# Feed-forward blocks that begin token-stationary, and a norm tile turned inside the output projection

## The reference

```
def rms_norm(x, g):
    y = x * rsqrt(mean(x * x, axis=-1, keepdims=True) + 1e-6)
    return y * g

def swiglu(h, w_in, w_out):                 # w_in: 1024 x 5632, w_out: 2816 x 1024
    a, b = split(h @ w_in, 2, axis=-1)
    return (silu(a) * b) @ w_out

for l in range(2):
    x = x + 0.5 * rms_norm(swiglu(rms_norm(x, ffn1_norm_pre[l]), ...), ffn1_norm_post[l])
    y = token_mixer(rms_norm(x, mix_norm_pre[l]), ...)       # ends in merged @ w_out
    x = x + rms_norm(y, mix_norm_post[l])
    x = x + 0.5 * rms_norm(swiglu(rms_norm(x, ffn2_norm_pre[l]), ...), ffn2_norm_post[l])
```

## Time and profile before

| | |
|---|---|
| median of 3 runs | 2048.53 us (2047.55 to 2050.34) |
| profiled execution | 2049.0 us |
| its span | 2047.3 us |
| TensorE busy | 1926.9 us, 94% |
| DVE, ScalarE, POOL busy | 1068.4, 899.9, 456.1 us |
| mean granted TensorE clock | 0.944 |

### The profile page before, as it was taken

The page is one execution under the profiler, slowest core; times in us unless marked ns, Lnnn a source line. Parts: engine busy times, 40 slices in busy tenths (PEclk is TensorE's granted clock), DMA queues, the critical chain, the costliest instruction groups (busy, mean ns, idle before and its releaser), DMA issues. The chain is left out here.

```text
span 2047.3 us, 31499 instructions
## 1 busy us (share of the span) xinstructions
PE 1926.9 (94%) x12048; PEld 1678.0 (82%) x12048; DVE 1068.4 (52%) x1887; ACT 899.9 (44%) x1386; POOL 456.1 (22%) x203
## 2 busy tenths in 40 slices
PE   6999999999899979999999999899888988999889
PEld 6999799988599969998999886899877867755665
DVE  7555561336355555554642344655484496651762
ACT  5443442784344444444335862444444433233363
POOL 1000001445100010000004443000066972004730
PEclk9999997999899979999997999899989998599999
DMA  6554446233354434544554324455434542004421
GB/s 275 185 184 184 174 177 241 99 124 124 134 185 184 184 135 179 185 185 170 186 214 156 118 97 150 168 184 186 157 124 149 190 154 93 1 1 151 157 93 52
DMA packets 29913, 311.69 MB, mean 152 GB/s; under 512 B 3312, under 2 KB 3696, under 8 KB 4848
## 3 DMA queue, kind: packets, MB, share of 16 engines
q1 hardware_dynamic: 28944, 307.13, 40.5%
q0 software_dynamic: 864, 3.15, 0.5%
HBM read 309.21 MB, written 1.05 MB: 152 GB/s over the span
## 5 line engine op out<-in xcount | busy, mean ns | idle before, releaser
L732 PE MATMUL psum<-hH,ring_r 128*128 128x256 f32 x2432 | 699.9, 288 | 0.0
L732 PE MATMUL psum<-hH,region_r 128*128 128x256 f32 x2336 | 668.4, 286 | 27.9 <-DVE xs_r L406 12.7
L732 PE MATMUL psum<-xs_r,region_r 128*128 128x256 f32 x2336 | 669.2, 286 | 0.0
L394 ACT ACTIVATE region_r<-ring 128x1024 fp32r<-128x1024 f32 x455 | 475.0, 1057 | 395.9 <-PE psum L732 341.9
L400 POOL TENSOR_TENSOR ring_r<-ring,region_r 128x1024 fp32r<-128x1024 f32 x141 | 344.5, 2466 | 1023.7 <-ACT region_r L394 1023.7
L400 DVE TENSOR_TENSOR ring_r<-ring,region_r 128x1024 fp32r<-128x1024 f32 x314 | 382.1, 1224 | 268.1 <-ACT region_r L394 252.1
L732 PEld LDWEIGHTS psum<-hH,region_r 128*128 128x128 f32 x2336 | 458.0, 196 | 42.6 <-issue 25.5
L732 PEld LDWEIGHTS psum<-hH,ring_r 128*128 128x128 f32 x2432 | 463.5, 191 | 0.0
L732 PEld LDWEIGHTS psum<-xs_r,region_r 128*128 128x128 f32 x2336 | 447.2, 191 | 4.4 <-issue 0.5
L732 PE MATMUL psum<-region_r 128*128 128x512 f32 x704 | 232.1, 392 | 0.0
L732 PE MATMUL psum<-region_r,hH 128*128 128x512 f32 (+3 forms) x512 | 160.4, 351 | 9.4 <-POOL ring_r L400 6.6
(11 more groups left out here) (200 smaller groups left out, 2138.9 us busy)
## 6 DMA issues: line engine op xcount, KB each, us to landing
ring<-in_weights SPq DMA_DIRECT2D x192, 1536.0 KB, 6.4
gpost<-in_posts POOLq DMA_DIRECT2D x6, 512.0 KB, 4.6
cst<-in_const SPq DMA_DIRECT2D x1, 1198.0 KB, 23.1
xs<-in_mem SPq DMA_DIRECT2D x1, 1024.0 KB, 5.6
x<-in_x SPq DMA_DIRECT2D x1, 1024.0 KB, 7.6
out<-x SPq DMA_DIRECT2D x2, 512.0 KB, 2.6
pars<-in_par SPq DMA_DIRECT2D x1, 336.0 KB, 8.0
p<-in_par SPq DMA_DIRECT2D x1, 204.0 KB, 24.8
```

The lines of the kernel that those rows point to most:

```text
L394: eng.activation(unit.high, unit.raw, ACT.Copy).then_inc(h_ready, 1)
L732: ins = pe.matmul(bank, lhsT, rhs, start=start, stop=stop)
```

## The change

The first two gate and up tiles of each block are computed by token tile: the normed tokens are the stationary operand and 512 columns (two gate tiles, two up tiles) move. `rows(i, some)` does this for token tile i. The host packs the first four units of a block accordingly. Gate and up then have tokens in partitions, so the product of Silu and up is turned by two transposes per token tile (`turned`), and DVE splits what comes out (`first_parts`). `first_down(i)` is the down product of hidden tile 0 for token tile i. The semaphore for hL is one per token tile, so that rows(0) does not wait for token tile 1. In first blocks, tile 1 is turned after half of rows(0); in second blocks, tile 0 is turned inside the output projection between kk = 4 and kk = 5 of token tile 1, and tile 1 after rows(0). AHEAD is 4.

(Cut to its core; headings of the hunks are put in words.)

```diff
@@ constants
-AHEAD = 2
+AHEAD = 4
...
@@ Jobs.ffn
+        for i in range(NT):
+            self.add("T", "gT", f, i)
...
@@ input_low (one semaphore per token tile)
-                .then_inc(nL_ready, 1)
+                .then_inc(nL_ready[i], 1)
...
@@ TensorE, ffn
-                norm(("ffn", f), k)
-                parted(k - 1)
+                if f == 0:
+                    norm(("ffn", f), k, [0])
...
-                up(0)
-                up(1)
-                down(0, first=True)
+                both = [Job("ff", f, i) for i in range(NT)]
+
+                def rows(i, some):
+
+                    for kk in some:
+                        unit = Split(at + kk // 2)
+                        if i == 0:
+                            pe.wait_ge(l_ready, unit.count)
+                        if kk % 4 == 0:
+                            pe.wait_ge(nL_ready[i], 2 * (k - 1) + kk // 4 + 1)
+                        if kk == 0:
+                            both[i].wait_empty(pe)
+                        products(both[i].bank, [h[:, i, kk, :] for h in (hH, hL)],
+                                 [w[:, kk % 2 * 512:(kk % 2 + 1) * 512] for w in (unit.high, unit.low)],
+                                 kk == 0, kk == KD - 1, both[i].full if kk == KD - 1 else None)
+                        if i and kk % 2:
+                            used.append(h_room)
+                        if i and kk == 5:
+                            used.append(w_used[at // 3 % SLOTS])
+
+                def turned(i):
+
+                    both[i].wait_emptied(pe)
+                    job = Job("gT", f, i)
+                    job.wait_empty(pe)
+                    for t in range(2):
+                        turn(job.bank[:, t * P:(t + 1) * P], gT[:, i, t * P:(t + 1) * P], job.full if t else None)
+
+                def first_down(i):
+                    Job("gT", f, i).wait_emptied(pe)
+                    unit = Split(at + 4)
+                    pe.wait_ge(l_ready, unit.count)
+                    for half in range(2):
+                        outs[2 * i + half].wait_empty(pe)
+                        products(outs[2 * i + half].bank, [g[:, 0, i * P:(i + 1) * P] for g in (gH, gL)],
+                                 [w[:, half * 512:(half + 1) * 512] for w in (unit.high, unit.low)],
+                                 True, False, h_room if i and half else None)
+
+                rows(0, range(0, 4))
+                if f == 0:
+                    norm(("ffn", f), k, [1])
+                rows(0, range(4, 8))
+                if f == 1:
+                    norm(("ffn", f), k, [1])
+                rows(1, range(0, 4))
+                turned(0)
+                rows(1, range(4, 8))
+                first_down(0)
+                turned(1)
+                first_down(1)

...
@@ TensorE, end of mixer, and project
-                project("mixed", AT_OUT, KD, mergedT, lambda kk: pe.wait_ge(merged, KD * lay[0] + kk + 1))
+                project("mixed", AT_OUT, KD, mergedT, lambda kk: pe.wait_ge(merged, KD * lay[0] + kk + 1),
+                        lambda: norm(("ffn", 1), k + 1, [0]))
...
+            def project(name, at, k, lhs, before, between=None):
+
+                project_rows(name, at, k, lhs, before, 0, range(k))
+                if between is None:
+                    project_rows(name, at, k, lhs, before, 1, range(k))
+                else:
+                    project_rows(name, at, k, lhs, before, 1, range(0, 5))
+                    between()
+                    project_rows(name, at, k, lhs, before, 1, range(5, k))
...
@@ ScalarE, ffn and end of mixer
-                norm_parts(("ffn", f))
+                if f == 0:
+                    norm_parts(("ffn", f))
                 first = U_FFN2 if f else U_FFN1
                 split(first, AHEAD, HIGHS)
                 table(ACT.Silu)
...
                 for i in range(NT):
                     post("mixed", 1.0, [i])
                     norm(k + 1, tiles=[i])
+                    norm_parts(("ffn", 1), [i])
...
@@ DVE, ffn (norm takes tiles now)
-                norm(("ffn", f), k, gain, scale="late" if f else "early")
+                if f == 0:
+                    norm(("ffn", f), k, gain, scale="early")
...
-                if f == 0:
-                    dve.tensor_tensor(hmT, memT, bc(A("gmem"), 2, SEQ), ALU.mult).then_inc(hm_ready, 1)
+                def first_gated(i):
+
+                    job = Job("ff", f, i)
+                    before = lay[0] * (2 * FT) + (f * FT + i)
+                    dve.wait_ge(sil_ready, before + 1)
+                    dve.tensor_tensor(gT[:, i, :], sil[:, i, :], job.bank[:, SEQ:2 * SEQ], ALU.mult).then_inc(job.free, 1)
+
+                def first_parts(i):
+
+                    job = Job("gT", f, i)
+                    before = lay[0] * (2 * FT) + (f * FT + i)
+                    cols = slice(i * P, (i + 1) * P)
+                    job.wait_full(dve)
+                    for t in range(2):
+                        dve.tensor_copy(gH[:, t, cols], job.bank[:, t * P:(t + 1) * P]).then_inc(g_steps, 1)
+                    dve.wait_ge(g_steps, 2 * before + 2)
+                    dve.tensor_tensor(gL[:, :, cols], job.bank[:, 0:SEQ].rearrange("p (t n) -> p t n", t=2),
+                                      gH[:, :, cols].bitcast(F32), ALU.subtract).then_inc(job.free, 1)

...
                 def body(it):
                     for c in range(SLOTS):
-                        gated(c, it)
                         for n in range(3):
                             low_part(dve, first + HIGHS + 3 * c + n, it)
-
+                        gated(2 + c, it)
+
+                first_gated(0)
+                first_parts(0)
+                first_gated(1)
+                first_parts(1)
+                if f == 0:
+                    dve.tensor_tensor(hmT, memT, bc(A("gmem"), 2, SEQ), ALU.mult).then_inc(hm_ready, 1)
                 repeat(dve, (FT - 2) // SLOTS, body)
-                gated(FT - 2)
-                gated(FT - 1)
+
...
@@ DVE, end of mixer
                 for i in range(NT):
                     post("mixed", p, 1, lay[0] + 1, [i])
-                    if i == 0:
-                        scaled(0, k + 1)
+                    scaled(i, k + 1)
+                    norm(("ffn", 1), k + 1, A("g2"), tiles=[i])
...
@@ host packing of the feed-forward weights
-        tiles = [a[0], b[0], a[1], b[1], o[0]]
+        both = [np.concatenate([t[:, k * P:(k + 1) * P] for t in (a[0], a[1], b[0], b[1])], 1) for k in range(KD)]
+        tiles = [np.concatenate(both[k:k + 2], 1) for k in range(0, KD, 2)] + [o[0]]
```

More of the change, by code:

```diff
@@ L549, in build @@
         h_room = sem("h_room")
-        nH_ready, nL_ready = sem("nH_ready"), sem("nL_ready")
+        nH_ready, nL_ready = sem("nH_ready"), [sem(f"nL_ready{i}") for i in range(NT)]
         yH_ready, yL_ready = sem("yH_ready"), sem("yL_ready")
@@ L753, in chunk_round, with norm @@
                 return n // SLOTS
-            def norm(name, k):
-                for i in range(NT):
+            def norm(name, k, tiles=range(NT)):
+                for i in tiles:
                     pe.wait_ge(xs_ready, NT * k + i + 1)
@@ L776, in parted @@
             def parted(k):
-                pe.wait_ge(nL_ready, 4 * (k + 1))
+                for i in range(NT):
+                    pe.wait_ge(nL_ready[i], 2 * (k + 1))
             def products(out, lhs, rhs, start, stop, signal=None):
@@ L820, in up, with down @@
                     used.append(h_room)
-                def down(t, it=0, first=False, last=False):
+                def down(t, it=0, last=False):
                     Job("ff", f, t, plus=2 * it).wait_emptied(pe)
@@ L828, in down @@
                         i, half = j // 2, j % 2
-                        if first:
-                            out_job.wait_empty(pe)
                         products(out_job.bank, [g[:, t % 2, i * P:(i + 1) * P] for g in (gH, gL)],
                                  [w[:, half * 512:(half + 1) * 512] for w in (unit.high, unit.low)],
-                                 first, last, out_job.full if last else h_room if j == 3 else None)
+                                 False, last, out_job.full if last else h_room if j == 3 else None)
@@ L1111, in project_rows @@
                         used.append(w_used[(at + kk // 3) % SLOTS])
-            def project(name, at, k, lhs, before):
-                for i in range(NT):
-                    project_rows(name, at, k, lhs, before, i, range(k))
+            def project(name, at, k, lhs, before, between=None):
[6 more added lines that the diff above has]
+                    project_rows(name, at, k, lhs, before, 1, range(5, k))
             def token_blocks(name, blocks, at):
@@ L1339, in split, with norm_parts @@
                     high_part(act_, u)
-            def norm_parts(name):
-                for i in range(NT):
+            def norm_parts(name, tiles=range(NT)):
+                for i in tiles:
```

(13 more changed lines are left out.)

## The result

Median of four runs 2073.5 us (2072.4 to 2073.8) against 2048.5 us: 1.012 times the time of before, 95% interval 1.0102 to 1.0137. The change costs 25.0 us; 27.7 were forecast. The profiled execution took 2073.3 us, its span is 2071.4, 24.1 longer than before's.

What follows compares the result with a forecast made beforehand. TensorE, busy 94% of the span, was taken as the bound, so its work and gaps counted. 4.0 + 10.0 + 2.2 + 10.0 + 1.5 = +27.7 us on 2048.5 gave 2076 us, range 2066 to 2088.

Steps and rivals of the forecast that it cites:

- Second blocks: Feed-forward blocks f = 1: ScalarE awaits the fourth unit's chunk before tile 0's post norm, TensorE stands 12 us; +10.0 us per layer.
- p: Time the low clock takes from a block's first products: 1.4 to 2.3 us, taken as equal before and after.
- silu(0)'s multiply: Multiply after tile 0's Silu, which turned(0) waits for: done at T + 5.9; in second blocks put at 571.9.
- T: The end of tile 1's transposes, from which silu(0)'s multiply is counted; 565.6 in the second block.
- Rival A: Second blocks: chunk lands before post("mixed") is due, so ScalarE is not held; -4.7 us per block, 2047 us in all; 8%.
- Rival B: Second blocks: TensorE at half clock over all six projection matmuls (+4) and again for rows(1) (+1 net); 2086 us; 10%.
- the wait for silu(0): TensorE's idle time before turned(0) in second blocks: 1.6 us, absorbing most of the loss from rows(1)'s half-clock start.
- First block of layer 0: Start 1.1 us late from two more POOL lows, plus 2.9 us for the block itself; together +4.0 us.
- The wait of first_down(1): TensorE idle behind turned(1) while DVE makes two copies and a subtraction: 1.15 us.
- Passage into layer 1: Four ScalarE highs delay the chain 1.5 us, yet the block starts 0.7 us early; with its +2.9, +2.2 us.
- Rival C: Steady loop: DVE's new order makes each up wait 0.2 to 0.5 us in 80 tiles; 2092 to 2116 us; 3%.
- the tail: Ahead of the even layer: the same four ScalarE highs as at layer 1's passage, with TensorE idle; +1.5 us.

Runs made afterwards that it cites:

- e1: Changed kernel, but in second blocks ScalarE makes three weight highs before tile 0's post norm and the fourth after it, POOL's lows likewise: 2044.2 us, 0.9982 of before.
- e2: Kernel before the change with one edit, AHEAD = 4 instead of 2, none of the new order: 2064.0 us, 1.0082 of before.
- e3: Changed kernel, but in first blocks and the even layer POOL makes two weight lows before norm_low and the other two behind: 2068.7 us, 1.0105 of before.
- e5: Changed kernel with the three reorderings of e1, e3 and e6 together: 2037.0 us, 0.9954 of before.
- e7: As e5, but DVE copies the turned tile out of PSUM in one 256-column copy instead of two of 128: 2038.6 us, 0.9960 of before.
- e4: Changed kernel, but second blocks turn tile 0 behind the whole output projection, the late weight high kept: 2062.3 us, 1.0068 of before.
- e6: Changed kernel, but at each layer's end ScalarE makes two weight highs before the post norm and the other two behind it: 2067.7 us, 1.0102 of before.

## Why the prediction was right

**Second blocks, the deciding step.** Forecast +10.0 each. Measured in layer 0: 13.21 us late at the third tile less 3.56 at the projection, +9.7. The steps, with after's times less 3.56 and the forecast behind them: transposes in the projection 548.7 (548.9); rows(0) 557.0 (557.1); tile 1's transposes 564.8 (564.5); its rows 567.6 (567.5). ScalarE began the high 6.29 us after the load's issue (the forecast had 6.0 to 6.6). The cause was named from one row, SP's issue at 534.49, together with the order of ScalarE's instructions, and e1 and e2 show it. In layer 1 the block cost 8.8 us: 15.8 late before the projection, 24.65 at the last Silu. The 1.2 us less than forecast are mostly on the side of before. From first product to Silu its block there took 8.59 us against 7.76 in layer 0, while after's two took 13.74 and 13.73; p, the low clock's share, was 2.6 us in that block of before and 1.8 in layer 0's.

The forecast's working has a slip here. It has silu(0)'s multiply done at 571.9, where its own T + 5.9 gives 571.5; measured was T + 5.7 (569.41 to 575.10). Without it the block would have come to +9.6.

**Rival A** was priced at 4.7 us gained per second block if the load were not in the way. e1 takes it out of the way and gains 5.2 in layer 0 and 4.7 in layer 1. Its mechanism and price were right, its condition (the slot free 6 us earlier) does not hold in this kernel.

**Rival B** held in part: the rest of the projection took 7.11 us at 554.00 against 5.32 in e1, so the low clock took 1.8 us, against 4 by the rival and about 1 in the forecast, and rows(1) started low once more. The window over rows(1):

```profile
571.00:575.00 4.00, 3.86 (x10) 3.04 (x11) 3.37 (x5) 3.97 (x6) 0.00 (x0) 0.57 0.01 2
```

That loss lies ahead of the wait for silu(0) and is hidden by it for the most part, as forecast: the block's cost came out 0.3 below.

**First block of layer 0: forecast +4.0, measured +5.2.** The start was 1.36 us late (forecast 1.1). The block took 3.8 us more, not 2.9 (the terms as listed add up to 2.8). The step that failed is "p stands on both sides and cancels". From 26.73 to 31.99 twelve matmuls of 512 columns take 5.26 us where 2.77 were due: p is 2.5 us and was 1.4. In layer 1 p is 2.5 against 2.25, and there the block took 2.89 more, as forecast. Layer 1's second block, above, is the same step with the other sign. The wait of first_down(1), put at 1.15 us, is 1.04.

**Passage into layer 1: forecast +2.2 less the block's 2.9, that is a start 0.7 us early; measured: 0.3 us later** (13.5 after 13.2). ScalarE's post norm comes 5.6 us behind the last Silu instead of 4.2: 1.4, forecast 1.5. The missing 1.0 is DVE's residual adds, 2.20 and 1.67 us where before had 1.26 and 1.22, beside POOL's four lows. The prediction charged POOL's lows for their own time and not for what they do to DVE. e3 shows both adds at 1.23 with the other two lows moved away. The Trainium skill (GPSIMD Engine Reference, "Specifications") lists POOL's SBUF interfaces as shared with VectorE, with contention where an instruction of DVE has two SBUF inputs. The rows agree: the residual add reads x and xs, both in SBUF. That entry gives no size, and here it was 0.45 to 0.94 us on 1.26.

**Rival C** is out: between the third tile and the last Silu no block gains or loses more than 0.02 us.

**The sum.** Forecast 4.0 + 10.0 + 2.2 + 10.0 + 1.5 = 27.7. Measured by the same stretches: 5.2, then -1.6 in layer 0's mixer, +9.7, +3.2, -0.6 in layer 1's mixer, +8.8, and -0.5 behind: 24.2, and the spans differ by 24.1. So layer 0's first block and the stretch from its second block to layer 1's third tile were 2.2 us too small in the forecast. Against that stand three things that it had too large or not at all: the two mixers gave back 2.2 us, layer 1's second block was 1.2 us cheaper, and the tail came out 2.0 below its +1.5. That the total is only 2.7 off is in part luck; the 20 us for the second blocks, 18.5 measured, are not.

The mixers. In layer 0 the lateness falls from 5.2 to 3.5 us between 332 and 337 us of before. There TensorE's granted clock is 0.50 in before from 332.1 on, and in after from 339.2 on; the low stretch lasts 30.7 us in before and 27.3 in after. The same window of both kernels, before first:

```profile
332.00:367.00 35.00, 34.09 (x173) 33.12 (x173) 4.84 (x17) 8.41 (x19) 6.25 (x3) 0.56 0.56 218
```
```profile
332.00:367.00 35.00, 34.09 (x191) 33.32 (x190) 3.02 (x13) 9.38 (x19) 6.26 (x3) 0.61 0.64 244
```

TensorE is equally busy in both, with 18 matmuls more in after at a mean clock of 0.61 against 0.56. Whether the change did this is not shown, and e5 and e7 speak against it: their mixers are the same program, and the low stretch in layer 0 lasts 27.3 us in one and 30.7 in the other. Layer 1's mixer gave back 0.6 us (16.4 late, then 15.8).

The tail. The +1.5 us forecast ahead of the even layer is not found at the end. Its products start 2.6 us later than before relative to the last Silu, yet this is gone later in the tail, and at the end 0.5 us less than at that Silu is left. The stretch from the last Silu to the end varies from 570.0 to 576.2 us over the seven experiments, and by 1.9 between e5 and e7, so this last term stays open.

## What to carry to other kernels

Here each engine takes its instructions in program order, so a deeper look-ahead can hold up what is queued behind it, as ScalarE's wait of 14.96 us held up the post norm. Before raising such a count, find the buffer slot that the extra item lands in, the instruction that frees it, and what stands behind the wait for it. If that is a chain that another engine needs, put the extra item behind the chain and keep the depth. Splitting the look-ahead of the second blocks (three, then one) turned a change that cost 25 us into one that gains 4; the two further reorderings bring the gain to 11. Moved work is not free either: the lows that e3 took out of one DVE instruction's way stood in another's at the next place. Where a transpose is put inside a stream of matmuls, the rest of the stream waits with it when its input is late (4.4 us in e4's comparison).

## What the runs showed of the hardware

- An add of DVE with both operands in SBUF, 128x1024, takes 1.23 us, and 1.67 to 2.20 us when it starts while a POOL subtraction of that size runs. It ends 1.08 to 1.09 us after that subtraction (after: POOL's ends at 760.50 and 763.80, the adds' at 761.58 and 764.88; e6: 762.26 and 763.35), nearly as if it began only then. DVE's input lows of 128x512, 0.7 us each alone, ended 0.54 to 0.55 us after POOL's subtraction (e3: 1512.85 and 1513.40, 1515.60 and 1516.14) and took 2.8 us each.
- After a wait of 8.9 us TensorE's 512-column matmuls started 0.43 us apart for 5.26 us, twice their 0.231. The window of after reads 1.00 there, because its clock has no record before 32.0 us. In e1 the same twelve matmuls run at the same pace, and there the clock is recorded as 0.50 from 18.0 to 31.7 us. In after's layer 1 the same pace goes with 0.50. The windows, after, e1 and after again:

```profile
26.70:32.00 5.30, 5.27 (x13) 4.04 (x14) 0.00 (x0) 0.00 (x0) 1.77 (x2) 1.00 0.52 193
...
26.70:32.00 5.30, 5.16 (x13) 4.04 (x14) 0.00 (x0) 0.00 (x0) 1.89 (x3) 0.54 0.51 198
...
774.00:779.40 5.40, 5.24 (x12) 4.04 (x13) 0.00 (x0) 0.00 (x0) 1.77 (x3) 0.50 0.30 97
```

- TensorE, busy for 34.1 of 35 us in layer 0's mixer, was granted 0.50 for 30.7 us in before and e7 and for 27.3 in after and e5.
- One 256-column copy out of PSUM takes 0.42 us on DVE (e7), two of 128 columns 0.49 together: halving the count saved 0.07 us.
